# The first modulation of a two-layer backbone, computed chunk by chunk, with three weight tiles in the first product

## The chip, the cores and the metric

One Trainium2 chip, one of its cores, one launch. The time is the device time of one execution in microseconds; three executions of the kernel before gave 1885.32, 1886.90 and 1889.01 us, a median of 1886.9 us. A core has five engines that run at once and wait for each other by semaphores: TensorE (PE), VectorE (DVE), ScalarE (ACT), GpSimd (POOL) and SyncE (SP). SyncE and GpSimd issue the loads here, SyncE on the hardware DMA queue and GpSimd on the software one.

## The reference, cut to what matters

Two layers work on 512 latent tokens and 256 context tokens, each of 1024 channels. The part of the first layer that the change touches:

```python
def rms_norm(x, g):
    y = xf * lax.rsqrt(jnp.mean(xf * xf, axis=-1, keepdims=True) + EPS)
    return (y * g.astype(F32)).astype(x.dtype)

def modulate(h, shift, scale):
    return h * (1 + scale) + shift

sh1, sc1, gt1, sh2, sc2, gt2 = split(silu(c) @ w_ada[l] + b_ada[l])      # latent tokens, w_ada: 1024 x 6144
csh1, csc1, ...              = split(silu(c_ctx) @ w_ada[l] + b_ada[l])  # context tokens, the same weights
u  = modulate(rms_norm(x, g_pre_mix[l]), sh1, sc1) @ w_in[l]             # w_in: 1024 x 2816, 22 tiles of 128 columns
uc = modulate(rms_norm(h_ctx, g_pre_mix[l]), csh1, csc1) @ w_in[l]
```

Behind it come four mixers (neighbourhood attention, a Fourier mixer, sliding-window attention, a gated recurrence), an output projection, and a gated feed-forward part. All is float32.

## The kernel before, in words

**Layout.** Channels lie on the partitions, 128 to a chunk, so that the 1024 channels are NC = 8 chunks; the 768 tokens lie along the rows, 512 latent and then 256 context. The transposed stream is in `x`. A weight tile is 1024 x 128: eight blocks of 128 x 128, 512 KB. There are 196 weight tiles in the whole kernel, in one order, `tile_source` says which.

**A product.** Each float32 product is made of three passes of a fast format: ScalarE copies the loaded tile `raw` into `w_hi` (the rounded part, `split_hi`), VectorE subtracts to get `w_lo` (the rest, `split_lo`), and the activations are split likewise in `h_hi` and `h_lo`. TensorE does hi x hi, lo x hi and hi x lo (`passes`), each in two matmuls of 384 tokens: 6 matmuls for one chunk of one tile, 48 for a tile. `raw`, `w_hi` and `w_lo` have RING = 3 slots, and SyncE loads tile k when the product of tile k - 3 is done (`stream`, L423). The products use the PSUM banks `ps[0]` and `ps[1]` in turn. The first two tiles of the first projection are done side by side (`side_by_side`): for each chunk, as soon as it is there, first tile 0, then tile 1. From the third on, a tile is done in one go.

**The first modulation.** Shift and scale of the first norm are 16 units (8 of shift, 8 of scale), each a row block of 128 x 1024 weights. A unit is a reduction on VectorE (`tensor_tensor_reduce`, L1517) of the weights with silu(c), and one with silu(c_ctx): 32 reductions, one after the other, with their main output thrown away in `ps[3]`. The weights come in ADA_FIRST = 8 transfers of two neighbouring units (1 MB each), so the first four transfers are all the shifts and the last four all the scales. SyncE issues c (two transfers, broadcast to all partitions), five of the eight, the first three weight tiles, and then waits until the first half of x is there before it issues the last three (L415). GpSimd issues the constants, waits for the first modulation transfer, and then issues x in two halves, five small tables, and the first two units of the modulation that comes later (`ada_w`, L492 to L503).

**ScalarE at the start** (from L746): silu of c; the first halves of weight tiles 0 and 1; then, when the small tables and x are there, `pre_norm`: eight squares of x, with the sum over channels made by TensorE (L851, `mean_square`), the root (L698, L699), and then for each chunk and each of the two token groups the copy into `h_hi` with the shift added (L713).

**VectorE at the start** (from L1506): the 32 reductions, the second halves of tiles 0 and 1 (L1521), then `pre_norm`: the columns of shift and scale (three small instructions, L1191 and L1202), and eight chunks of scaling into `tmp` (L1211, two instructions a chunk) and of making `h_lo` (L1218, two a chunk). The split of chunk c - 1 comes behind the scaling of chunk c, so that ScalarE can make `h_hi` beside. Then `ada_pair(0)`, which are four reductions of the later modulation units (L1151) and a small copy, and `gate_bounds`, nine small instructions. Then `projections`: for b from 0 to 7, the split of tile b + 2 (L1139) and, up to b = 6, `ada_pair(b + 1)`; then the recurrence's work, in steps that are fixed to the progress of the product (`STEPS`). GpSimd reloads `ada_w` for a pair when the reductions of the pair before have read it (`ada_loads`, L472).

The order on each engine is the order in which the program writes its instructions; nothing reorders them.

Of the kernel before, what the change touches and what calls it, by code (L numbers as in the profile page):

```python
# [20 lines left out]
F32 = mybir.dt.float32  # L21
# [29 lines left out]

RING = 3
N_OUT = NC

# [94 lines left out]
def hybrid_kernel(nc, xT, cvec, wstream, adaT, badaT, gT, rpb, wf, sink, lbT, hgT, dftL, dftC, dftD, rotm,  # L149
                  rope, swamask, namask, lvmask, sqc, out):  # L150
    with ExitStack() as ctx:
# [241 lines left out]
        def tile_source(k):  # L393
# [6 lines left out]
            return k  # L400

        STEPS = [steps_after(l) for l in range(DEPTH)]

# [5 lines left out]
        def _(sp):  # L409
            for v in range(2):  # L410
                sp.dma_start(c_b[:, v], bass.AP(cvec.tensor, v * D, [[0, P], [1, D]])).then_inc(s_cin, 16)
            for k in range(ADA_FIRST):
                if k == ADA_FIRST // 2 + 1:
                    sp.wait_ge(x_ld[0], 16)
                sp.dma_start(first_units(k), adaT[2 * k:2 * k + 2].rearrange("u p d -> p u d")).then_inc(ada_0_ld[k], 16)  # L415
                if k == ADA_FIRST // 2:
                    for u in range(RING):
                        sp.dma_start(raw[:, u], wstream[tile_source(u)]).then_inc(raw_ld[u], 16)
# [48 lines left out]
        def _(pool):  # L467
# [24 lines left out]
            pool.dma_start(consts[:], sqc.rearrange("k p n -> p k n")).then_inc(s_in, 16)  # L492
            pool.wait_ge(ada_0_ld[0], 16)
            for k in range(2):
# [55 lines left out]
        def _(act):  # L550
# [23 lines left out]
            def project(l, b):  # L574


                blk = PROJ_ORDER[b]
                T = block_width(l, blk)
                act.wait_ge(blk_done, 2 * TP[l]["proj"] + b + 1)
                act.activation(as_product(u_t[:, blk, 0:T], T), product_of(ps[b % 2], T),  # L580
                               ACT.Silu if blk >= QD else ACT.Copy).then_inc(bank_free[b % 2], 1)

            def projections(l):
                g0 = 2 * TP[l]["proj"]
                for b in range(N_ALONE):
                    split_hi(g0 + b + 2)
                    project(l, b)
                steps = recurrence(l)
                for b in range(N_ALONE, N_PROJ):
                    for k in range(NC):  # L590
                        if k == NC // 2 and b < N_PROJ - 1:
                            split_hi(g0 + b + 2)
                        for _ in range(STEPS[l][b][k]):
                            next(steps)
                    project(l, b)
                    if b == N_PROJ - 1:
                        split_hi(g0 + b + 2)
                    if PROJ_ORDER[b] == GD + 1:
                        act.preload_act_table_set(ROOT_TABLES)
# [107 lines left out]
            def pre_norm(T, ready):  # L707
                mean_square(x, T, ready)
                for c in range(NC):
                    for lo, hi, v in STREAMS[:2 if T == TOK else 1]:  # L710
                        act.wait_ge(scaled, nn[0] + 1)
                        nn[0] += 1
                        act.activation(h_hi[:, c, lo:hi], tmp[:, c % 2, lo:hi], ACT.Identity,  # L713
                                       bias=col_sh[:, c, v:v + 1]).then_inc(hhi_ready, 1)
# [33 lines left out]
            act.preload_act_table_set(ROOT_TABLES)  # L748
            for u in range(2):
                act.wait_ge(raw_ld[u], 16)  # L750
                act.activation(w_hi[:, u].rearrange("p c n -> p (c n)"), raw[:, u], ACT.Copy).then_inc(w_hi_done, 1)

            for l in range(DEPTH):
                tp, T = TP[l], width[l]
                if l == 0:
                    act.wait_ge(s_in, 16 * 6)
                    act.wait_ge(consts_done, 1)
                    pre_norm(TOK, lambda c: act.wait_ge(x_ld[2 * c // NC], 16))

# [33 lines left out]
        def _(pe):  # L793
            def passes(tile, k, rhs_hi, rhs_lo, T, begin, end):

                u, slot = tile % 2, tile % RING
                for w, r, first, last in ((w_hi, rhs_hi, begin, False), (w_hi, rhs_lo, False, False),
# [4 lines left out]

            def side_by_side(g0, rhs_hi, rhs_lo, kc, T, ready, order):


                for u in range(2):
                    pe.wait_ge(w_lo_done, 2 * g0 + u + 1)
                    pe.wait_ge(bank_free[u], g0 + 1)
                for n, k in enumerate(order):
                    ready(n)  # L810
                    for u in range(2):
                        mm = passes(2 * g0 + u, k, rhs_hi, rhs_lo, T, n == 0, n == kc - 1)
                        if n == kc - 1:
                            mm.then_inc(blk_done, 1)
# [13 lines left out]
            def projections(l, ready):  # L828


                g0 = TP[l]["proj"]
                side_by_side(g0, h_hi, h_lo, NC, TOK, ready, range(NC))
                steps = recurrence(l)
                for b in range(2, N_PROJ):
                    pe.wait_ge(w_lo_done, 2 * g0 + b + 1)
# [291 lines left out]
        def _(dve):  # L1127
# [68 lines left out]
            nrs, nhi, nlo, nm, nx = [0], [0], [0], [0], [0]  # L1196

            def pre_norm(l, sh, sc, g, T):

# [3 lines left out]
                nrs[0] += 1  # L1203
                dve.wait_ge(rstd_ready, nrs[0])
                st = STREAMS[:2 if T == TOK else 1]
                for c in range(NC + 1):
                    if c >= 2:
                        dve.wait_ge(hlo_ready, nlo[0])
                    if c < NC:
                        for lo, hi, v in st:  # L1210
                            dve.scalar_tensor_tensor(tmp[:, c % 2, lo:hi], x[:, c, lo:hi], col_gs[:, c, v:v + 1],  # L1211
                                                     rstd[:, lo:hi], ALU.mult, ALU.mult).then_inc(scaled, 1)
                    if c:
                        for lo, hi, v in st:
# [150 lines left out]
            def projections(l):  # L1365
                g0 = TP[l]["proj"]
                for b in range(N_ALONE):
                    split_lo(2 * g0 + b + 2)
                    if l == 0 and b < N_ALONE - 1:
# [140 lines left out]
            dve.wait_ge(s_cb, 1)  # L1510
            for k in range(2 * ADA_FIRST):
                if k % 2 == 0:
                    dve.wait_ge(ada_0_ld[k // 2], 16)
                for v in range(2):
                    if 2 * k + v:
                        dve.wait_ge(ada_0_done, 2 * k + v)
                    dve.tensor_tensor_reduce(ps[3][:], first_units(k // 2)[:, k % 2], c_b[:, v], 1.0, 0.0, ALU.mult,  # L1517
                                             ALU.add, ada_c[0][:, k, v:v + 1]).then_inc(ada_0_done, 1)
            for u in range(2):
                dve.wait_ge(w_hi_done, u + 1)  # L1520
                dve.tensor_tensor(w_lo[:, u].rearrange("p c n -> p (c n)"), raw[:, u],  # L1521
                                  w_hi[:, u].rearrange("p c n -> p (c n)").bitcast(F32), ALU.subtract)\
                   .then_inc(w_lo_done, 1)
            dve.wait_ge(s_in, 16 * 6)
            for k in range(2):
                dve.wait_ge(x_ld[k], 16)
            dve.wait_ge(ada_0_done, 4 * ADA_FIRST)

            for l in range(DEPTH):
                tp, T = TP[l], width[l]  # L1530
                if l:
                    dve.wait_ge(ada_copied, 41)
                pre_norm(l, SH1, SC1, G_PRE_MIX, TOK)
                if l == 0:
                    ada_pair(0)
# [130 lines left out]
```

## Time and profile before

| what | value |
|---|---|
| median of three runs | 1886.9 us (1885.32 to 1889.01) |
| the profiled execution's own time | 1888.17 us |
| its span in the profile | 1886.3 us |
| TensorE matmul busy | 1721.2 us, 91% |
| VectorE busy | 978.9 us, 52% |
| ScalarE busy | 597.3 us, 32% |
| GpSimd busy | 148.9 us, 8% |
| mean granted TensorE clock | 0.959 of full speed |
| moved by DMA | 178.84 MB, mean 95 GB/s |

The shares are averages over the whole span. The change touches only the first 150 us or so, in which the engines stand otherwise: in the page's first of 40 slices (47 us) VectorE is busy 7 tenths of the time, TensorE 1 tenth, and the DMA engines 8 tenths, at 329 GB/s. Idle time in a row stands in square brackets, with what ended it behind the arrow. A granted clock of 1.00 is 2.4 GHz, 0.50 is 1.2 GHz.

### The profile page before, as it was taken

Reading aid. Unit: us, or ns where it says so; the run is one execution under the profiler, and the core shown is the slowest. Engines: PE = TensorE matmul, PEld = TensorE weight load, DVE = VectorE, ACT = ScalarE, POOL = GpSimd, SP = SyncE. Lnnn points to the kernel's source line nnn. Section 1 sums busy time; section 2 is a strip of 40 time slices with the busy share of each in tenths; the row PEclk is TensorE's granted clock in tenths of the full one; section 3 lists DMA queues with packets and bytes.
Section 4 is the critical chain, followed back from the end, with each engine's and each line's share of the span. In section 5 each row is a group of like instructions: output and inputs, shape, how many; then the busy total and the mean of one; then the engine's idle time right before and its main releaser. Section 6 shows DMA issues by size and latency. Waiting matters only on the chain.

```text
span 1886.3 us, 24628 instructions
## 1 busy us (share of the span) xinstructions
PE 1721.2 (91%) x10460; PEld 1510.4 (80%) x10460; DVE 978.9 (52%) x1603; ACT 597.3 (32%) x796; POOL 148.9 (8%) x186
## 2 busy tenths in 40 slices
PE   2699998899889999999999979899799899999996
PEld 1699986559689999999999959797566587887874
DVE  7978426665475554555654371752852532233334
ACT  2334434442342222221122142543462432332231
POOL 1010001003200000000000400000102000000003
PEclk9799998899999999999999989999889899999998
DMA  8261115212124343443432202114401132332322
GB/s 329 87 200 47 57 38 124 106 44 71 65 67 134 123 127 111 131 127 109 136 120 89 73 17 79 46 57 95 117 1 56 48 97 90 100 91 92 97 90 100
DMA packets 80638, 178.84 MB, mean 95 GB/s; under 512 B 38912, under 2 KB 39424, under 8 KB 80272
## 3 DMA queue, kind: packets, MB, share of 16 engines
q1 hardware_dynamic: 66864, 122.70, 21.2%
q0 software_dynamic: 13664, 54.56, 8.4%
q8 instruction: 83, 1.36, 0.3%
q14 instruction: 27, 0.22, 0.0%
HBM read 175.14 MB, written 2.10 MB: 94 GB/s over the span
## 4 chain that ended last, share of the span: by engine, by line
PE 82%; DVE 11%; DMA 3%; ACT 2%; issue 1%; SPq 1%; DVEq 0%; ACTq 0%
PE psum L800 70%; PE psum L927 2%; PE psum L938 2%; DMA ada_0a<-in_adaT 1%; DVE f_t L1233 1%; DVE s_sb L1279 1%; PE psum L961 1%; PE psum L1019 1%; DVE x L1237 1%; SPq L441 1%; PE psum L851 1%; DVE tmp L1211 1%; PE psum L883 1%; DVE psum L1517 1%; DMA raw<-in_wstream 1%
## 5 line engine op out<-in xcount | busy, mean ns | idle before, releaser
L800 PE MATMUL psum<-h_hi,w_hi 128*128 128x384 f32 (+1 forms) x1872 | 556.0, 356 | 32.3 <-DVE h_lo L1218 26.6
L800 PE MATMUL psum<-h_hi,w_lo 128*128 128x384 f32 (+1 forms) x1872 | 546.6, 351 | 0.0
L800 PE MATMUL psum<-h_lo,w_hi 128*128 128x384 f32 (+1 forms) x1872 | 546.3, 351 | 0.0
L1139 DVE TENSOR_TENSOR w_lo<-raw,w_hi 128x1024 fp32r<-128x1024 f32 x194 | 239.4, 1234 | 384.2 <-ACT w_hi L562 383.2
L800 PEld LDWEIGHTS psum<-h_hi,w_hi 128*128 128x128 f32 x1872 | 342.1, 190 | 59.2 <-issue 31.6
L562 ACT ACTIVATE w_hi<-raw 128x1024 fp32r<-128x1024 f32 x194 | 205.6, 1060 | 506.3 <-DMA raw<-in_wstream 506.1
L800 PEld LDWEIGHTS psum<-h_lo,w_hi 128*128 128x128 f32 x1872 | 345.5, 190 | 19.9 <-issue 0.7
L800 PEld LDWEIGHTS psum<-h_hi,w_lo 128*128 128x128 f32 x1872 | 344.9, 189 | 19.8
L1151 DVE CUSTOM_DVE_ANT_0 psum<-ada_w,c_b 128x1024 f32<-128x1024 f32 x160 | 202.3, 1264 | 12.0 <-DMA ada_w<-in_adaT 3.3
L800 PE MATMUL psum<-hid_hi,w_hi 128*128 128x384 f32 (+1 forms) x528 | 161.9, 361 | 15.5 <-DVE w_lo L1139 13.2
L1179 DVE TENSOR_TENSOR tmp<-tmp,psum 128x768 f32<-128x768 f32 (+1 forms) x44 | 36.1, 821 | 266.0 <-PE psum L800 266.0
L800 PE MATMUL psum<-hid_hi,w_lo 128*128 128x384 f32 (+1 forms) x528 | 160.9, 359 | 0.0
L800 PE MATMUL psum<-hid_lo,w_hi 128*128 128x384 f32 (+1 forms) x528 | 160.9, 359 | 0.0
L800 PEld LDWEIGHTS psum<-hid_hi,w_hi 128*128 128x128 f32 x528 | 98.5, 192 | 27.3 <-DVE w_lo L1139 17.3
L800 PEld LDWEIGHTS psum<-hid_hi,w_lo 128*128 128x128 f32 x528 | 98.9, 192 | 7.3
L800 PEld LDWEIGHTS psum<-hid_lo,w_hi 128*128 128x128 f32 x528 | 98.8, 192 | 7.0
L851 PE MATMUL psum<-sq,consts 128*128 128x512 f32 (+1 forms) x112 | 49.5, 597 | 53.0 <-ACT sq L692 53.0
L472 POOL DMA_DIRECT2D ada_w<-in_adaT x78 | 41.3, 530 | 707.3 <-DVE ada_t L1151 706.7
L851 PEld LDWEIGHTS psum<-sq,consts 128*128 128x128 f32 x112 | 23.5, 224 | 78.6 <-issue 49.7
L486 POOL TENSOR_TENSOR sq<-f_t 128x768 f32<-128x768 f32 (+1 forms) x28 | 41.1, 1467 | 561.6 <-DVE f_t L1166 449.4
L738 ACT ACTIVATE s_sb<-s_sb,nb 128x512 f32<-128x512 f32 (+3 forms) x80 | 56.8, 714 | 47.9 <-DVE nb L1286 33.7
L682 ACT ACTIVATE hid_hi<-tmp 128x768 fp32r<-128x768 f32 (+1 forms) x44 | 32.5, 740 | 120.6 <-DVE tmp L1179 120.6
(167 smaller groups left out, 1451.0 us busy)
## 6 DMA issues: line engine op xcount, KB each, us to landing
raw<-in_wstream SPq DMA_DIRECT2D x196, 512.0 KB, 3.6
ada_w<-in_adaT POOLq DMA_DIRECT2D x80, 512.0 KB, 3.9
ada_0a<-in_adaT SPq DMA_DIRECT2D x6, 1024.0 KB, 14.6
x<-in_xT POOLq DMA_DIRECT2D x4, 1536.0 KB, 14.3
na_r<-in_rpb SPq DMA_DIRECT2D x64, 64.0 KB, 3.5
fn_l<-in_dftL POOLq DMA_DIRECT2D x2, 2048.0 KB, 8.4
ada_0b<-in_adaT SPq DMA_DIRECT2D x2, 1024.0 KB, 19.3
out_xT<-x SPq DMA_DIRECT2D x4, 512.0 KB, 2.8
```

The lines of the kernel that those rows point to most:

```text
L472: pool.dma_start(ada_w[:, u], adaT[2 * ADA_ORDER[q] + (2 * ADA_FIRST + u)]).then_inc(ada_ld[u], 16)
L486: link(pool.tensor_tensor(sq[:, 1 if b == 0 else 0, 0:T], f, f, ALU.mult))
L562: act.activation(w_hi[:, k % RING].rearrange("p c n -> p (c n)"), raw[:, k % RING], ACT.Copy)\
L682: act.activation(hid_hi[:, i, 0:T], tmp[:, 1, 0:T], ACT.Copy).then_inc(hid_hi_done, 1)
L738: act.activation(p, p, ACT.Exp, bias=nb[:, s % 3, j:j + 1], scale=SCALE, accum_out=sums[:, s % 3, j:j + 1]).then_inc(at_p, 1)
L800: mm = pe.matmul(ps[u][:, at:at + hi - lo], w[:, slot, k], r[:, k, lo:hi], start=first, stop=last)
L851: mm = pe.matmul(ps[2][:, lo:hi], ones, sq[:, c % 2, lo:hi], start=c == 0, stop=c == NC - 1)
L927: mm = pe.matmul(dst, q, keys, start=True, stop=True)
L938: mm = pe.transpose(pt_ps[:, n * j + P * c:n * j + P * c + P], s_sb[:, v % 3, j, o:o + P], ident)
L1139: dve.tensor_tensor(w_lo[:, k % RING].rearrange("p c n -> p (c n)"), raw[:, k % RING], w_hi[:, k % RING].rearrange("p c n -> p (c n)").bit ...
L1151: dve.tensor_tensor_reduce(ps[3][:], ada_w[:, u], c_b[:, v], 1.0, 0.0, ALU.mult, ALU.add, ada_t[:, u, v:v + 1]).then_inc(ada_done, 1)
L1179: dve.tensor_tensor(as_product(tmp[:, 1, 0:T], T), as_product(tmp[:, 0, 0:T], T), product_of(ps[1], T), ALU.mult).then_inc(bank_free[1], 1)
```

## The change

A transfer of the first modulation now holds the shift unit and the scale unit of the same chunk, so that a chunk can be modulated when its own transfer has been reduced. VectorE takes reductions and norm in turn: four transfers are reduced, the three first weight tiles split, and the chunks 0 to 3 normed; then two transfers and chunks 4 and 5; then one and chunk 6; then one and chunk 7. The first product handles three tiles side by side instead of two, the third in the bank `ps[2]`, which no tile used before. ScalarE makes the squares and the root ahead of the first parts of the weight tiles, and of three tiles instead of two. GpSimd doesn't wait any more for the first modulation transfer before it loads x, and SyncE doesn't wait for x before the last three modulation transfers.

```diff
+N_FIRST = 3
+        def bank_of(k):
+            return k if k < N_FIRST else k % 2
@@ block.sync
             for k in range(ADA_FIRST):
-                if k == ADA_FIRST // 2 + 1:
-                    sp.wait_ge(x_ld[0], 16)
-                sp.dma_start(first_units(k), adaT[2 * k:2 * k + 2].rearrange("u p d -> p u d")).then_inc(ada_0_ld[k], 16)
+                sp.dma_start(first_units(k), adaT[k:k + NC + 1:NC].rearrange("u p d -> p u d")).then_inc(ada_0_ld[k], 16)
                 if k == ADA_FIRST // 2:
-                    for u in range(RING):
+                    for u in range(N_FIRST):
                         sp.dma_start(raw[:, u], wstream[tile_source(u)]).then_inc(raw_ld[u], 16)
@@ block.gpsimd
             pool.dma_start(consts[:], sqc.rearrange("k p n -> p k n")).then_inc(s_in, 16)
-            pool.wait_ge(ada_0_ld[0], 16)
             for k in range(2):
@@ block.scalar, projections
                 for b in range(N_ALONE):
-                    split_hi(g0 + b + 2)
+                    if l or b + 2 >= N_FIRST:
+                        split_hi(g0 + b + 2)
                     project(l, b)
@@ block.scalar, the start
-            for u in range(2):
-                act.wait_ge(raw_ld[u], 16)
-                act.activation(w_hi[:, u].rearrange("p c n -> p (c n)"), raw[:, u], ACT.Copy).then_inc(w_hi_done, 1)
-
...
-                    pre_norm(TOK, lambda c: act.wait_ge(x_ld[2 * c // NC], 16))
+                    mean_square(x, TOK, lambda c: act.wait_ge(x_ld[2 * c // NC], 16))
+                    for u in range(N_FIRST):
+                        split_hi(u)
+                    normed(TOK)
@@ block.tensor
-                for u in range(2):
+                for u in range(tiles):
                     pe.wait_ge(w_lo_done, 2 * g0 + u + 1)
-                    pe.wait_ge(bank_free[u], g0 + 1)
+                    pe.wait_ge(bank_free[u % 2], g0 + 1)
                 for n, k in enumerate(order):
                     ready(n)
-                    for u in range(2):
+                    for u in range(tiles):
...
-                side_by_side(g0, h_hi, h_lo, NC, TOK, ready, range(NC))
+                first = 2 if l else N_FIRST
+                side_by_side(g0, h_hi, h_lo, NC, TOK, ready, range(NC), first)
@@ block.vector
+            def first_norm():
+                done = 0
+                for k in range(ADA_FIRST):
+                    dve.wait_ge(ada_0_ld[k], 16)
+                    for part in range(2):
+                        for v in range(2):
+                            n = 4 * k + 2 * part + v
+                            if n:
+                                dve.wait_ge(ada_0_done, n)
+                            dve.tensor_tensor_reduce(ps[3][:], first_units(k)[:, part], c_b[:, v], 1.0, 0.0, ALU.mult,
+                                                     ALU.add, ada_c[0][:, (SH1, SC1)[part] + k, v:v + 1])\
+                               .then_inc(ada_0_done, 1)
+                    if k < 3 or k == 4:
+                        continue
+                    if k == 3:
+                        dve.wait_ge(s_in, 16 * 6)
+                        for u in range(N_FIRST):
+                            split_lo(u)
+                        for half in range(2):
+                            dve.wait_ge(x_ld[half], 16)
+                        nrs[0] += 1
+                        dve.wait_ge(rstd_ready, nrs[0])
+                    dve.wait_ge(ada_0_done, 4 * k + 4)
+                    part = slice(done, k + 1)
+                    b = [bada[:, 0, at0 + done:at0 + k + 1].unsqueeze(2).to_broadcast([P, k + 1 - done, 2])
+                         for at0 in (SH1, SC1)]
+                    g = gcol[:, 0, G_PRE_MIX, part].unsqueeze(2).to_broadcast([P, k + 1 - done, 2])
+                    dve.tensor_tensor(col_sh[:, part], ada_c[0][:, SH1 + done:SH1 + k + 1], b[0], ALU.add)
+                    link(dve.tensor_tensor(col_sc[:, part], ada_c[0][:, SC1 + done:SC1 + k + 1], b[1], ALU.add))
+                    link(dve.scalar_tensor_tensor(col_gs[:, part], col_sc[:, part], 1.0, g, ALU.add, ALU.mult))
+                    normed(TOK, done, k + 1)
+                    done = k + 1
...
-                for c in range(NC + 1):
-                    if c >= 2:
+                for c in range(c0, c1 + 1):
+                    if c >= c0 + 2 or c0:
                         dve.wait_ge(hlo_ready, nlo[0])
-                    if c < NC:
+                    if c < c1:
...
-                    if c:
+                    if c > c0:
@@ block.vector, projections
                 for b in range(N_ALONE):
-                    split_lo(2 * g0 + b + 2)
+                    if l or b + 2 >= N_FIRST:
+                        split_lo(2 * g0 + b + 2)
                     if l == 0 and b < N_ALONE - 1:
                         ada_pair(b + 1)
@@ block.vector, the start
-            for k in range(2 * ADA_FIRST):
...
-            for u in range(2):
-                dve.wait_ge(w_hi_done, u + 1)
...
+            first_norm()
...
-                pre_norm(l, SH1, SC1, G_PRE_MIX, TOK)
-                if l == 0:
+                if l:
+                    pre_norm(l, SH1, SC1, G_PRE_MIX, TOK)
+                else:
                     ada_pair(0)
                     gate_bounds()
```

## Rows read from the trace of the kernel before

**Rows 1.** The page's part 4: shares of the chain that ended last.
```profile
PE 82%; DVE 11%; DMA 3%; ACT 2%; issue 1%; SPq 1%; DVEq 0%; ACTq 0%
```

**Rows 2.** The chain in order of time, 0 to 160: start us, length us, what.
```profile
81.99 1.24 DVE w_lo L1139
83.27 53.40 PE psum L800 x294
```

**Rows 3.** Timeline of VectorE: start us, us, engine line op, out<-in xcount [idle before].
```profile
10.20 1.23 DVE L1517 CUSTOM_DVE_ANT_0 psum<-ada_0a,c_b 128x1024 f32<-128x1024 f32 x1 [9.33 <-DMA ada_0a<-in_adaT]
...
15.61 1.23 DVE L1517 CUSTOM_DVE_ANT_0 psum<-ada_0a,c_b 128x1024 f32<-128x1024 f32 x1
...
55.95 0.17 DVE L1191 TENSOR_TENSOR col_sh<-ada_c,bada 128x16 f32<-128x16 f32 x1
...
56.57 2.21 DVE L1211 SCALAR_TENSOR_TENSOR tmp<-x,col_gs,rstd 128x512 f32<-128x512 f32 x4
...
72.14 2.33 DVE L1218 SCALAR_TENSOR_TENSOR h_lo<-tmp,col_sh,h_hi 128x512 fp32r<-128x512 f32 x4
74.50 1.23 DVE L1151 CUSTOM_DVE_ANT_0 psum<-ada_w,c_b 128x1024 f32<-128x1024 f32 x1
...
81.58 0.16 DVE L1504 TENSOR_TENSOR lb<-lbt,lb 128x4 f32<-128x4 f32 x1
...
83.13 1.23 DVE L1151 CUSTOM_DVE_ANT_0 psum<-ada_w,c_b 128x1024 f32<-128x1024 f32 x1
...
88.62 1.22 DVE L1139 TENSOR_TENSOR w_lo<-raw,w_hi 128x1024 fp32r<-128x1024 f32 x1
...
132.69 1.23 DVE L1139 TENSOR_TENSOR w_lo<-raw,w_hi 128x1024 fp32r<-128x1024 f32 x1 [0.89 <-ACT w_hi L562]
```

**Rows 4.** Timeline of TensorE, at full clock: 27 pairs start between these two.
```profile
88.67 0.51 PE L800 MATMUL psum<-h_hi,w_hi 128*128 128x384 f32 x2
...
98.03 0.51 PE L800 MATMUL psum<-h_hi,w_hi 128*128 128x384 f32 x2
```

**Rows 5.** Windows: stretch and its us, busy us of PE, PEld, DVE, ACT, POOL, PEclk, DMA, GB/s.
```profile
83.20:88.00 4.80, 4.73 (x15) 4.73 (x16) 4.59 (x8) 2.04 (x3) 0.53 (x1) 0.50 0.44 137
83.27:135.30 52.03, 52.03 (x288) 52.03 (x288) 46.09 (x73) 12.64 (x14) 7.40 (x14) 0.95 0.62 201
```

**Rows 6.** Timeline of GpSimd at the start: constants, the two of x, last small table.
```profile
1.25 0.92 POOL L492 DMA_DIRECT2D consts<-in_sqc  x1 [0.81 <-POOLq L1659]
10.35 1.53 POOL L496 DMA_DIRECT2D x<-in_xT  x2 [8.18 <-DMA ada_0a<-in_adaT]
...
14.01 0.54 POOL L501 DMA_DIRECT2D hgain<-in_hgT  x1
```

**Rows 7.** DMA queues: packets, MB, share; in 0:6.5, 0:10.05, 14:16, 16:26 (two rows).
```profile
q1 hardware_dynamic: 389, 1.46, 63.2%
...
q1 hardware_dynamic: 731, 2.80, 73.5%
...
q0 software_dynamic: 66, 0.41, 49.5%
...
q0 software_dynamic: 415, 2.45, 61.2%
q1 hardware_dynamic: 418, 1.59, 40.3%
```

**Rows 8.** DMA issues at 14.01 and at 77.4: count, KB each, us to landing.
```profile
hgain<-in_hgT POOLq DMA_DIRECT2D x1, 2.0 KB, 16.0
...
ada_w<-in_adaT POOLq DMA_DIRECT2D x1, 512.0 KB, 4.6
```

**Rows 9.** Timeline of ScalarE: a weight split, the first squares, the root's last step.
```profile
30.20 1.06 ACT L751 ACTIVATE w_hi<-raw 128x1024 fp32r<-128x1024 f32 x1 [20.78 <-DMA raw<-in_wstream]
...
33.72 1.56 ACT L692 ACTIVATE sq<-x 128x768 f32<-128x768 f32 x2
...
48.96 0.84 ACT L699 ACTIVATE rstd<-lnms 128x768 f32<-128x768 f32 x1
```

More of the change, by code:

```diff
@@ L579, in project @@
                 act.wait_ge(blk_done, 2 * TP[l]["proj"] + b + 1)
-                act.activation(as_product(u_t[:, blk, 0:T], T), product_of(ps[b % 2], T),
+                act.activation(as_product(u_t[:, blk, 0:T], T), product_of(ps[bank_of(2 * TP[l]["proj"] + b)], T),
                                ACT.Silu if blk >= QD else ACT.Copy).then_inc(bank_free[b % 2], 1)
@@ L708, in pre_norm, with normed @@
                 mean_square(x, T, ready)
+                normed(T)
+            def normed(T):
                 for c in range(NC):
@@ L794, in passes @@
             def passes(tile, k, rhs_hi, rhs_lo, T, begin, end):
-                u, slot = tile % 2, tile % RING
+                u, slot = bank_of(tile), tile % RING
                 for w, r, first, last in ((w_hi, rhs_hi, begin, False), (w_hi, rhs_lo, False, False),
@@ L801, in passes, with side_by_side @@
                 return mm
-            def side_by_side(g0, rhs_hi, rhs_lo, kc, T, ready, order):
-                for u in range(2):
+            def side_by_side(g0, rhs_hi, rhs_lo, kc, T, ready, order, tiles=2):
+                for u in range(tiles):
                     pe.wait_ge(w_lo_done, 2 * g0 + u + 1)
-                    pe.wait_ge(bank_free[u], g0 + 1)
+                    pe.wait_ge(bank_free[u % 2], g0 + 1)
                 for n, k in enumerate(order):
                     ready(n)
-                    for u in range(2):
+                    for u in range(tiles):
                         mm = passes(2 * g0 + u, k, rhs_hi, rhs_lo, T, n == 0, n == kc - 1)
@@ L831, in projections @@
                 g0 = TP[l]["proj"]
-                side_by_side(g0, h_hi, h_lo, NC, TOK, ready, range(NC))
+                first = 2 if l else N_FIRST
+                side_by_side(g0, h_hi, h_lo, NC, TOK, ready, range(NC), first)
                 steps = recurrence(l)
-                for b in range(2, N_PROJ):
+                for b in range(first, N_PROJ):
                     pe.wait_ge(w_lo_done, 2 * g0 + b + 1)
@@ L1204, in pre_norm, with normed @@
                 dve.wait_ge(rstd_ready, nrs[0])
+                normed(T, 0, NC)
+            def normed(T, c0, c1):
                 st = STREAMS[:2 if T == TOK else 1]
-                for c in range(NC + 1):
-                    if c >= 2:
+                for c in range(c0, c1 + 1):
+                    if c >= c0 + 2 or c0:
                         dve.wait_ge(hlo_ready, nlo[0])
-                    if c < NC:
+                    if c < c1:
                         for lo, hi, v in st:
@@ L1510, in _ @@
             dve.wait_ge(s_cb, 1)
-            for k in range(2 * ADA_FIRST):
[L1512 to L1518, printed above, removed]
-            for u in range(2):
-                dve.wait_ge(w_hi_done, u + 1)
[L1521 to L1527, printed above, removed]
+            first_norm()
             for l in range(DEPTH):
```

## The prediction

> **What bounds the kernel now.** I read the shares of the chain that ended last first. The reader is to see that TensorE carries 82% of it and VectorE 11%: a change at the start is worth what it does to the moment from which TensorE runs without a gap [rows 1]. Then the chain in order of time: from 83.27 us TensorE runs 53.4 us in one piece of 294 matmuls, and what releases it is the second part of one weight tile, written by VectorE at 81.99 (L1139) [rows 2]. So all before 83.27 is set by VectorE, and one number measures the change: when the fourth weight tile (number 3) is through TensorE.
>
> Third, VectorE in order of time [rows 3]. From 10.20 it runs reductions of L1517, four for 1 MB of modulation weights, one such group each 15.61 - 10.20 = 5.4 us; eight groups, then two splits, end at 55.9. Then come the column sums (56.57 - 55.95 = 0.62 us), eight chunks of scaling and splitting (56.57 to 74.47: 2.24 us a chunk), ada_pair(0) and gate_bounds (74.50 to 81.74: 7.24 us), the split of tile 2, ada_pair(1) (83.13 to 88.62: 5.5 us), the split of tile 3. There is hardly a gap: the start is a queue of VectorE work, and its order decides.
>
> Fourth, TensorE. Side by side it takes tiles 0 and 1 while the chunks come, and stops before 83.27. A pair of matmuls takes (98.03 - 88.67)/27 = 0.347 us [rows 4], a tile of 24 pairs 8.32 us. The six tiles 2 to 7 took 52.03 us, 2.1 more than 6 x 8.32, and the row of the stretch after the restart shows a granted clock of 0.50 [rows 5]: half of full speed (1.2 GHz of 2.4) after the pause that [rows 2] ends. So now tile 2 ends at 83.27 + 10.4 = 93.7, tile 3 at 102.0.
>
> **The change part by part, on the profile's own time axis.**
>
> *Loads.* GpSimd no longer waits for the first modulation transfer, so the two transfers of x follow the constants at 1.25 + 0.92 = 2.2 us instead of 10.35, 8.15 earlier [rows 6]. SyncE no longer waits for x either. The bytes are the same; only who goes first changes. Transfers of x issued at 10.35 show up in the queue's bytes in the slice 14 to 16 us, with half of it, so about 4 us after issue; now from about 6.5. While both queues have work, the software queue moves 2.45 MB and the hardware queue 1.59 MB in 10 us: 0.245 and 0.159 MB/us [rows 7]. The last small table was issued at 14.01 and took 16.0 us; ScalarE needs all of them before it squares. Shifted by 8.15 it lands at 30.0 - 8.15 = 21.9 [rows 6, 8].
>
> The modulation chunks pay for it. Chunk 0 landed just before 10.20 [rows 3], when the hardware queue had moved 2.80 MB; the 1 MB of c and the chunk are 2, so a landing comes 0.8 MB late. Now 1.46 MB are through at 6.5, and 0.159 MB/us from there give chunk 0 at 6.5 + 1.34/0.159 = 14.9, chunk 1 at 21.2. The software queue's 4.3 MB (x 3.1, first ada_w tiles 1.05, tables) are through at 24.0; alone at 0.40 the hardware queue lands chunk 2 near 25.4 and chunk 3 near 27.9 [rows 7]. VectorE at 5.4 a chunk: 14.9 to 20.3, 21.2 to 26.6, to 32.0, to 37.5. It starts 4.7 late and has a gap of about 0.9.
>
> That row can be read in two ways. In it both queues moved as many packets, 415 and 418, but not as many bytes [rows 7]. The Trainium skill (DMA: Bandwidth & Descriptors, "Queues, rings and completion order") says that each DMA engine goes round its queues packet by packet; by that rule x keeps its advantage from the start, and the split by bytes that I used holds; by even bytes x would come 3 us later (a rival below). The trace agrees with the rule.
>
> *Order on ScalarE.* The squares now come ahead of the weight splits. The squares, their sums on TensorE and the root took 33.72 to 49.80 = 16.1 us, cold matmuls included [rows 9]. From 21.9 that ends at 38.0. Then three splits of 1.06 us [rows 9]: tile 0's first part is there at 39.05, the last by 41.0. VectorE has stood since 37.5, 1.6 us. Its three second parts (1.14 apart) end at 42.55. The weights themselves have long landed (before at 30 to 33 behind the same bytes), so nothing hides here but the wait for x.
>
> *Norm in four stretches.* From 42.55: columns 0.62 and chunks 0 to 3 at 2.24: 52.1. Chunks 4 and 5: reductions 10.8, columns 0.62, two chunks 4.5: 68.1. Chunk 6: 5.4 + 0.62 + a single chunk. A single one cannot overlap with its neighbour: 1.15 scaling + 1.14 split + ScalarE's part between. At least it costs the 2.24 of a chunk, at most 1.15 + 1.12 + 1.14 = 3.4; I take 2.8, since the narrow half overlaps: 76.9. Chunk 7 the same: 85.7. Before, the last chunk was ready at 74.47 [rows 3]: 11 us later, of which late start and stalls 7.2 (4.7 + 0.9 + 1.6), the third split moved ahead 1.1, three more sets of columns 1.9, bubbles 1.2; rounding the rest.
>
> *Three tiles side by side.* TensorE has 9 pairs a chunk, 3.1 us warm. It is idle before chunks 4 and 7 for 4 us and more, so it meets chunk 7 at half clock: (about 7 x 0.64 + 2 x 0.347) = 5.2, the 0.64 from the 2.1 us that seven pairs lost. Tiles 0, 1, 2 end at 91.0; before, tile 2 ended at 93.7. That is the gain that the change holds, 2.7 us, if the next tile is ready.
>
> *What the next tile waits for.* It is not. In the new order VectorE does after chunk 7: ada_pair(0) and gate_bounds 7.24: 92.95; the split in front of ada_pair(1) has gone, for tile 2 is split already; ada_pair(1), whose first weights land 4.6 us after an issue that follows the pair's start by 2.9, so 0.25 of wait [rows 8]: 93.2 to 98.7; only then tile 3's split, and TensorE 1.28 us after its start [rows 2]: 100.0. Beside it, hidden: the load of raw 3 is issued when tile 0 ends (about 87.9), lands by 93, ScalarE splits it by 94. If VectorE were free that would be the next thing late: 94 + 1.3 = 95.3. TensorE has idled 9 us, and restarts at half clock: tile 3 ends at 100.0 + 10.4 = 110.4.
>
> *After it* all is as before. Tiles 4 to 7 follow each 8.32; VectorE needs 132.69 - 88.62 = 44.1 us from tile 3's split to tile 9's, TensorE 52.03 - 8.32 = 43.7 from tile 3 to tile 8 with the restart; so VectorE is just in time, with under 1 us of slack where the recurrence starts [rows 3, 5]. Layer 1 is unchanged.
>
> **Sum.** Tile 3 ends at 110.4 instead of 102.0: +8.4 us. The profiled execution took 1888.17 (span 1886.3), so 1896.6 for one like it; it stands 1.3 above the median of 1886.9, so the median becomes 1895.3. 0.2% (3.8 us) is what a measurement here can tell from no change. Bounds: if VectorE alone set the pace (chunk 0 at 10.2, x in time), three splits would end at 10.2 + 21.7 + 3.5 = 35.4, 7.1 earlier: +1.3; with a warm restart besides, -0.8. If x lands 4 us later than I say: +12.4.
>
> **Rivals.**
> *The start is not slowed* (not slower): x and the chunks both come early enough that VectorE never stands. For it: the whole load of 14.6 MB is unchanged, and VectorE, not the queue, is the slower one now. Against: the root needs x by 35.4 - 3.5 - 16.1 = 15.8, that is nearly all of the bandwidth from 6.5 on, and then chunk 0 is late by the same bytes. Price: +1.3, so 1888.2. It decides if both ScalarE has its root and VectorE its fourth group by 32.
> *TensorE sets the end and gains*: tile 3's split would be ready by 91.0, 2.7 to 3 us faster: 1884. Against: ada_pair(1) stands before the split, and even the best start gives 92.9.
> *The queues share evenly by bytes*: 3.3 MB until x and the tables are in takes 16.3 us at 0.202 instead of 13.5 at 0.245, some 3 us later for ScalarE, while VectorE has its chunks earlier: +11.4, so 1898.3. Against: the row says otherwise.
> *Later work gives some back*: a wait behind tile 8 that is not tied to TensorE absorbs part, say half: +4.2, 1891.1. Against: all loads there are released by finished tiles.
>
> **How the numbers follow.** Forecast (+8.4, with sizes off by up to 2.5): 0.70. Even bytes or x later: 0.12. Later work gives back: 0.06. Start not slowed: 0.08. TensorE gains: 0.04. Slower by over 0.2%: 0.70 + 0.12 + half of the 0.06 = 0.85; within: 0.08 + 0.03 = 0.11; faster: 0.04. The range from 1889 to 1899.5 leaves out the faster case and the start that is hardly slowed, and the far end of late x.
>
> **What would show it.** In the new profile: chunk 0's first reduction near 15; ScalarE's first square near 22, its last root near 38; VectorE standing before its first split (near 37 to 39); reductions and scalings in turn until 85.7; then ada_pair(0), the gates and ada_pair(1) ahead of tile 3's split near 98.7; TensorE idle from 91 to 100 with that split as what ended it, clock 0.50 after it. Wrong would be: a first square before 18, the last chunk before 80, or tile 3 starting before 95.

## The result, and the profile after

The changed kernel takes 1895.3 us (median of five, 1892.4 to 1896.1) against 1886.9 (five, 1885.3 to 1889.0): ratio 1.0040, 95% interval [1.0026, 1.0055]. The medians differ by 8.4 us, as forecast to a tenth; the interval of the ratio allows anything from 4.9 to 10.4 us, so the tenth means nothing. The agreement is partly luck besides: the traces show a first stage that lost 12.5 us where 8.4 were forecast, and about 4 us that came back later.

The profiled execution took 1895.34 us (span 1893.5), which is the median itself. VectorE in order of time; columns as in [rows 3]:

```profile
12.53 1.23 DVE L1216 CUSTOM_DVE_ANT_0 psum<-ada_0a,c_b 128x1024 f32<-128x1024 f32 x1 [11.66 <-DMA ada_0a<-in_adaT]
...
18.88 1.23 DVE L1216 CUSTOM_DVE_ANT_0 psum<-ada_0a,c_b 128x1024 f32<-128x1024 f32 x1 [1.09 <-DMA ada_0a<-in_adaT]
...
41.10 3.50 DVE L1146 TENSOR_TENSOR w_lo<-raw,w_hi 128x1024 fp32r<-128x1024 f32 x3 [6.13 <-ACT w_hi L565]
...
53.95 1.23 DVE L1216 CUSTOM_DVE_ANT_0 psum<-ada_0a,c_b 128x1024 f32<-128x1024 f32 x1
...
75.37 1.15 DVE L1256 SCALAR_TENSOR_TENSOR tmp<-x,col_gs,rstd 128x512 f32<-128x512 f32 x2
76.98 1.15 DVE L1263 SCALAR_TENSOR_TENSOR h_lo<-tmp,col_sh,h_hi 128x512 fp32r<-128x512 f32 x2 [0.46 <-ACT h_hi L720]
78.16 1.23 DVE L1216 CUSTOM_DVE_ANT_0 psum<-ada_0b,c_b 128x1024 f32<-128x1024 f32 x1
...
86.72 1.23 DVE L1158 CUSTOM_DVE_ANT_0 psum<-ada_w,c_b 128x1024 f32<-128x1024 f32 x1
...
94.06 1.23 DVE L1158 CUSTOM_DVE_ANT_0 psum<-ada_w,c_b 128x1024 f32<-128x1024 f32 x1
...
99.73 1.23 DVE L1158 CUSTOM_DVE_ANT_0 psum<-ada_w,c_b 128x1024 f32<-128x1024 f32 x1 [3.05 <-DMA ada_w<-in_adaT]
...
102.46 1.22 DVE L1146 TENSOR_TENSOR w_lo<-raw,w_hi 128x1024 fp32r<-128x1024 f32 x1
...
147.46 1.22 DVE L1146 TENSOR_TENSOR w_lo<-raw,w_hi 128x1024 fp32r<-128x1024 f32 x1
...
150.02 0.96 DVE L1465 COPY hv<-psum 128x768 f32<-128x768 f32 x1
```

The reader is to see the brackets: 2.3 us later at the start, 1.09 for the second chunk, 6.13 before the first split, and 3.05 in the middle of ada_pair(1), which I had not in the sum. The last row is the recurrence's first work on VectorE. Before, it stood at 137.46 behind 2.24 us of waiting for TensorE; now it comes 12.6 later, straight behind the queue. The same row before:

```profile
137.46 0.96 DVE L1419 COPY hv<-psum 128x768 f32<-128x768 f32 x1 [2.24 <-PE psum L1031]
```

ScalarE beside it, as in [rows 9]: the squares start 10.1 us earlier than before, and the root is what the splits wait for.

```profile
23.64 1.58 ACT L696 ACTIVATE sq<-x 128x768 f32<-128x768 f32 x2 [13.71 <-DMA hgain<-in_hgT]
...
39.21 0.84 ACT L703 ACTIVATE rstd<-lnms 128x768 f32<-128x768 f32 x1
39.95 2.93 ACT L565 ACTIVATE w_hi<-raw 128x1024 fp32r<-128x1024 f32 x3
```

TensorE, as in [rows 4]: tile 2 in the kernel before, then chunk 7 of the three tiles and tile 3 in the changed one.

```profile
83.27 1.01 PE L800 MATMUL psum<-h_hi,w_hi 128*128 128x384 f32 x2 [4.49 <-DVE w_lo L1139]
```

```profile
86.74 1.01 PE L806 MATMUL psum<-h_hi,w_hi 128*128 128x384 f32 x2 [5.16 <-DVE h_lo L1263]
...
103.73 1.01 PE L806 MATMUL psum<-h_hi,w_hi 128*128 128x384 f32 x2 [11.10 <-DVE w_lo L1146]
```

Windows of the changed kernel, as in [rows 5]: from the restart at 103.73 the clock is 0.50 for some 5.5 us, and so it was from 86.7 on.

```profile
86.70:92.00 5.30, 5.26 (x16) 5.26 (x17) 5.07 (x8) 0.00 (x0) 0.53 (x1) 0.50 0.45 152
...
103.73:109.20 5.47, 5.47 (x17) 5.47 (x18) 4.96 (x8) 0.00 (x0) 0.53 (x1) 0.50 0.49 158
```

The prediction named one number, the end of tile 3 on TensorE. SyncE issues its next weight load then, here before and after: 12.5 us later, where 8.4 was forecast.

```profile
102.38 0.33 SPq L423 DMA_DIRECT2D raw<-in_wstream  x1
```

```profile
114.89 0.33 SPq L427 DMA_DIRECT2D raw<-in_wstream  x1
```

### The profile page after: what moved, and what is told of

Same layout as the page of the kernel before. It is cut to its first block, busy times and chain, and to the rows that moved or that the text cites. A ratio compares the mean times of both kernels' runs of the same rounds, so it can differ in the third digit from the quotient of the medians.

```text
span 1893.5 us, 24643 instructions
## 1 busy us (share of the span) xinstructions
PE 1722.5 (91%) x10460; PEld 1511.7 (80%) x10460; DVE 980.0 (52%) x1612; ACT 597.0 (32%) x796; POOL 149.0 (8%) x186
## 4 chain that ended last, share of the span: by engine, by line
PE 82%; DVE 11%; ACT 2%; DMA 2%; issue 1%; SPq 1%; POOL 0%; DVEq 0%; ACTq 0%; POOLq 0%
PE psum L806 69%; PE psum L934 2%; PE psum L945 2%; PE psum L858 2%; DVE f_t L1278 1%; DVE s_sb L1324 1%; PE psum L968 1%; PE psum L1026 1%; DVE psum L1216 1%; DMA hgain<-in_hgT 1%; DVE x L1282 1%; SPq L445 1%; DVE w_lo L1146 1%; DVE psum L1158 1%; PE psum L890 1%
```

## The experiments

In this table "recurrence" is the start of VectorE's first copy into `hv`, and "tile 16" how much later than in the first profile of the kernel before VectorE split weight tile 16 (207.1 us there), by which time the first steps of the recurrence are through.

| kernel | median us (runs) | ratio to before | recurrence | tile 16 |
|---|---|---|---|---|
| before, profiled first | 1886.9 | | 137.46 | 0 |
| before, again | 1886.6 (12) | 1.0007 [0.9997, 1.0017] | 138.36 | +0.9 |
| changed | 1895.3 (5) | 1.0040 [1.0026, 1.0055] | 150.02 | +12.5 |
| changed, again | 1895.5 (5) | 1.0046 [1.0029, 1.0063] | 150.36 | +12.2 |
| a: split 3 first | 1892.7 (9) | 1.0033 [1.0018, 1.0047] | 150.68 | +8.2 |
| b: five groups | 1891.3 (10) | 1.0027 [1.0017, 1.0037] | 145.26 | +6.5 |
| c: two tiles | 1894.1 (7) | 1.0040 [1.0025, 1.0055] | 147.81 | +10.3 |
| e: x late | 1901.1 (5) | 1.0078 [1.0064, 1.0093] | 154.63 | +16.4 |
| g: weights behind ada_w | 1892.8 (5) | 1.0033 [1.0021, 1.0045] | 149.96 | +8.9 |
| j: b and g | 1889.1 (11) | 1.0015 [1.0006, 1.0024] | 146.00 | +5.8 |
| d: before, loads early | 1890.1 (11) | 1.0013 [1.0003, 1.0023] | 140.58 | +3.1 |
| f: before, third split early | 1883.5 (11) | 0.9986 [0.9977, 0.9994] | 138.31 | -0.6 |
| k: f, gates first | 1885.7 (12) | 0.9996 [0.9987, 1.0006] | 139.44 | +2.0 |
| l: k, split 3 first | 1882.2 (12) | 0.9980 [0.9969, 0.9992] | 140.72 | -0.2 |

The intervals of a, b, c and g overlap those of the changed kernel, whose ten executions lie between 1892.1 and 1898.9 us; b's lie between 1888.8 and 1894.4. Only e and j are clear of it by their intervals, so what a, c and g are worth is read mainly from the traces.

**What the early x costs and brings.** Experiment e puts one wait back into the changed kernel:

```diff
             pool.dma_start(consts[:], sqc.rearrange("k p n -> p k n")).then_inc(s_in, 16)
+            pool.wait_ge(ada_0_ld[0], 16)
```

> The changed kernel with GpSimd waiting again for the first modulation transfer before it loads x. Theory 1 (x and the small tables set the root, the root sets the splits, and VectorE stands for it): chunk 0's reduction starts at 10.2 instead of 12.5, the first square near 32 instead of 23.6, VectorE stands from 32 to 49, and the time rises by about 8 us. Theory 2 (the early x is what slows the start, by taking half of the bandwidth): the time falls by 2 to 3 us.

```profile
9.60 1.23 DVE L1217 CUSTOM_DVE_ANT_0 psum<-ada_0a,c_b 128x1024 f32<-128x1024 f32 x1 [8.73 <-DMA ada_0a<-in_adaT]
...
45.81 1.23 DVE L1147 TENSOR_TENSOR w_lo<-raw,w_hi 128x1024 fp32r<-128x1024 f32 x1 [14.71 <-ACT w_hi L566]
```

Chunk 0 comes 2.9 us earlier and helps nothing; VectorE stands 14.71 us for the root, the splits are 4.7 later, and the median rises by 5.7. Theory 1 in kind; I had said 8, but the first square came at 29.7, not 32. So with the new order on ScalarE x has to come early. Experiment d takes the two waits out of the kernel before and leaves its order:

```diff
-            pool.wait_ge(ada_0_ld[0], 16)
...
-                if k == ADA_FIRST // 2 + 1:
-                    sp.wait_ge(x_ld[0], 16)
```

> The kernel before with one part of the change: GpSimd does not wait for the first modulation transfer, nor SyncE for x. Order of work, transfers and two tiles side by side stay. Theory 1 (the early x costs the first chunks what the change's trace shows, a start at 12.5 instead of 10.2 and 1.1 us more of waiting, less the 0.6 us gap that goes): about 2.8 us slower, all of it ahead of tile 2. Theory 2 (with x early ScalarE and the loads are ready sooner and this pays): no change or faster.

The first reduction starts at 12.83 and tile 2 at 86.39, 3.1 later than in [rows 2]; the median is 3.4 above the kernel before's 1886.7 (by the interval 0.6 to 4.3). The early x alone costs about what theory 1 said, in a kernel whose VectorE doesn't stand for the root.

**Where VectorE stands.** Experiment b:

```diff
-                    if k < 3 or k == 4:
+                    if k < 4:
                         continue
-                    if k == 3:
+                    if k == 4:
```

> The changed kernel with one edit: five groups of reductions instead of four before the first splits and norms (chunks 0 to 4, then 5, 6 and 7 singly). VectorE stood 6.1 us before the first split in the changed kernel, for ScalarE's root. Theory 1 (that stand is paid in full, all after it is one queue): 5.4 us of reductions fit into it, less 0.5 for one more single chunk, so 4.9 us faster, and the recurrence starts at 145. Theory 2 (TensorE's restarts or the ada_w loads set the pace behind it): under 2 us faster.

```profile
41.48 2.36 DVE L1146 TENSOR_TENSOR w_lo<-raw,w_hi 128x1024 fp32r<-128x1024 f32 x2 [1.19 <-ACT w_hi L565]
...
145.26 0.96 DVE L1465 COPY hv<-psum 128x768 f32<-128x768 f32 x1
```

The stand falls from 6.13 to 1.19 and the recurrence starts 4.8 earlier, where 4.9 was said; the median falls by 4.1. VectorE's stand is paid in full in the first stage.

**The second unit of ada_pair(1).** In the changed kernel it is issued at 92.39 and lands 7.3 us later, while SyncE issues three weight tiles (89.06, 90.98, 92.67), since three tiles end within 4 us. Experiment g, in SyncE's `stream`:

```diff
                     sp.wait_ge(blk_done, k - RING + 1)
+                    if k == RING + 1:
+                        sp.wait_ge(ada_ld[1], 32)
```

> The changed kernel with one edit: SyncE loads weight tile 4 (and 5 behind it) only when the second unit of ada_pair(1) has landed. Theory 1 (the three weight loads that the three finished tiles release within 4 us hold this unit up, it took 7.3 us to land and VectorE stood 3.05 us): the unit lands in 4.5 to 5 us, VectorE's wait there falls under 0.5 us, tile 3's split comes near 99.5 instead of 102.46, and the first stage is 2.5 to 3 us shorter. Theory 2 (the unit is late because GpSimd issues it late, at 92.39, whatever else is in flight): no change.

DMA issue of that unit in the kernel before, in the changed kernel, then in g (count, KB, us to landing):

```profile
ada_w<-in_adaT POOLq DMA_DIRECT2D x1, 512.0 KB, 5.1
```

```profile
ada_w<-in_adaT POOLq DMA_DIRECT2D x1, 512.0 KB, 7.3
```

```profile
ada_w<-in_adaT POOLq DMA_DIRECT2D x1, 512.0 KB, 3.8
```

```profile
99.24 1.22 DVE L1148 TENSOR_TENSOR w_lo<-raw,w_hi 128x1024 fp32r<-128x1024 f32 x1
...
102.30 1.23 DVE L1160 CUSTOM_DVE_ANT_0 psum<-ada_w,c_b 128x1024 f32<-128x1024 f32 x1 [1.84 <-issue]
```

The wait is gone and the split comes at 99.24 (102.46 in the changed kernel, 98.7 in the prediction). With the loads of tiles 4 and 5 held back the unit lands in half the time, so the transfers compete, and that is the missing term. VectorE's queue gets most of it back in later waits for `ada_w`, the recurrence starts where it did (149.96), yet tile 16 is 3.6 earlier: TensorE's lead counts also when VectorE's start does not move. The median is 2.6 lower, within the intervals. Experiment j has both edits, b and g.

> The changed kernel with two edits together: five groups of reductions ahead of the first norm, and weight tiles 4 and 5 loaded only behind the second unit of ada_pair(1). Theory 1 (the two are separate entries in one queue on VectorE, and add): 4.0 and 2.6 us off the changed kernel's median, so about 1888.7, 2 us above the kernel before. Theory 2 (one hides the other): not better than the better of the two, 1891.3.

1889.1, against 1888.7 if they add: the median favours theory 1, though b's and j's intervals overlap. The changed kernel with its two stands mended is still 0.15% slower than before. By the terms of the sum the rest would be the late start of the first splits, three more sets of columns, and short idle gaps; no run separates them.

**TensorE's wait or VectorE's queue.** Experiment a, in VectorE's `projections`:

```diff
-                    if l or b + 2 >= N_FIRST:
+                    if l:
                         split_lo(2 * g0 + b + 2)
+                    elif b < N_ALONE - 1:
+                        split_lo(b + 3)
                     if l == 0 and b < N_ALONE - 1:
                         ada_pair(b + 1)
```

> The changed kernel with one edit: VectorE splits tile 3 ahead of ada_pair(1), and every later tile of the eight ahead of its pair. Theory 1 (TensorE's wait for tile 3, 11.1 us in the changed kernel, is what the end pays): the split follows ScalarE's at 94.8, TensorE starts tile 3 at 96.1 instead of 103.73, and the time falls by about 7.6 us. Theory 2 (VectorE's whole queue up to the recurrence is the bound, since it came there at 149.99 and TensorE at 149.18, so that both are tied): TensorE gets to tile 8 7 us earlier but VectorE begins the recurrence at about 150 as before, TensorE's wait moves there, and the time falls by 0 to 2 us.

```profile
96.83 1.01 PE L806 MATMUL psum<-h_hi,w_hi 128*128 128x384 f32 x2 [3.59 <-DVE w_lo L1146]
...
142.44 0.82 PE L1038 MATMUL psum<-consts,u_t 128*128 128x128 f32 x6
```

```profile
150.68 0.96 DVE L1467 COPY hv<-psum 128x768 f32<-128x768 f32 x1
```

TensorE reaches the recurrence 6.6 us earlier, VectorE no earlier, and the result is neither theory's: 4.3 us by tile 16, 2.7 in the median. In the recurrence TensorE waits 2.2 us for VectorE once, where the changed kernel has no such wait, so a part of the lead is lost there. My reading, which no run tests by itself: the lead is product work that is done and not owed when VectorE's steps come, and is worth a part of itself. Experiment c goes back to two tiles (`N_FIRST = 2`, with RING weight tiles still loaded at the start).

> The changed kernel with two tiles side by side instead of three, all else the same. Theory 1 (the third tile puts tile 3's split behind two pairs, and three weight loads at once hold up ada_pair(1) by 3.05 us): tile 2 starts at 94.2 and the tiles then follow, tile 8 at 146.2 instead of 149.2, VectorE's wait of 3.05 us for ada_w is gone, and the time falls by 2 to 3 us. Theory 2 (the third tile is worth the 2.7 us that TensorE gains by it): the time rises by 2 to 3 us.

```profile
94.15 1.01 PE L806 MATMUL psum<-h_hi,w_hi 128*128 128x384 f32 x2 [4.54 <-DVE w_lo L1146]
...
147.81 0.96 DVE L1465 COPY hv<-psum 128x768 f32<-128x768 f32 x1 [1.96 <-PE psum L1038]
```

Tile 2 starts at 94.15 as said, the wait for `ada_w` is gone, the first stage is 2.2 shorter; the median is 1.2 lower, within both intervals. No gain of the third tile shows, and its cost is not resolved by times.

**What of the change is worth keeping.** Experiment f puts only the third split ahead of the norm, in the kernel before:

```diff
-            for u in range(2):
+            for u in range(3):
                 act.wait_ge(raw_ld[u], 16)
...
-            for u in range(2):
+            for u in range(3):
                 dve.wait_ge(w_hi_done, u + 1)
```

(and in `projections` on both engines the split at b = 0 of layer 0 is left out).

> The kernel before with one edit: ScalarE and VectorE split tile 2 together with tiles 0 and 1, ahead of the norm, so that TensorE need not wait from 78.8 to 83.3. Theory 1 (TensorE's wait is the price): tile 2 follows at once at 79.6 without a restart at half clock, tile 3's split comes at 88.4 behind ada_pair(1), tile 8 starts 4 us earlier, 4 us faster. Theory 2 (VectorE's queue up to the recurrence is the other bound, with 2.2 us of slack where it waited for TensorE at 137.46): at most 2.2 us faster.

```profile
83.35 0.98 PE L801 MATMUL psum<-h_hi,w_hi 128*128 128x384 f32 x2 [2.76 <-ACT u_t L580]
```

The split was in time, but TensorE stood all the same: ScalarE's copy of tile 0 out of its bank was queued behind the exponential that `gate_bounds` releases (82.30). Still it is the first version that beats both: 0.9986, or 2.6 us. Experiment k calls `gate_bounds` ahead of `ada_pair(0)`; l also has a's order of splits.

> The kernel before with the third weight split ahead of the norm, as in f_before_third_split_early, and gate_bounds ahead of ada_pair(0) on VectorE. In that run TensorE stood 2.8 us before tile 2, not for the split but for ScalarE's copy of tile 0 out of its bank, which was queued behind the small exponential that gate_bounds releases. Theory 1 (TensorE's earlier progress pays, as where tile 3's split was put first in the changed kernel): TensorE goes through at 80.6, without 2.8 us of standing and about 2 us of restart, and the time is 2 to 4 us below that run's 1883.5. Theory 2 (VectorE's queue to the recurrence, which starts at 138.3 in that run without waiting for TensorE, is the bound): no change from 1883.5.

> As k_gates_first, and each split of the eight ahead of its pair on VectorE (tile 3's ahead of ada_pair(1)). Theory 1: TensorE has tile 3 in time at 89 as well (in k it waits about 2 us for a split at 90 and restarts at half clock), so another 2 to 4 us, 1878 to 1881. Theory 2 (VectorE's queue is the bound): VectorE stands about 1.5 us for ScalarE before that split, the recurrence starts that much later, and it is not faster than k, or 1 us slower.

Timeline of TensorE in k, then the window 79 to 131 us of l (columns as in [rows 5]):

```profile
93.10 1.01 PE L801 MATMUL psum<-h_hi,w_hi 128*128 128x384 f32 x2 [5.03 <-DVE w_lo L1140]
```

```profile
79.00:131.00 52.00, 52.00 (x300) 51.76 (x300) 42.01 (x65) 15.11 (x16) 6.90 (x13) 1.00 0.63 203
```

In k the wait moved on: ada_pair(1) now follows so soon that it stands 3.5 us for its weights, tile 3's split comes at 91.8, and TensorE stands 5 us for it. Neither theory had that, and the median is 2.1 above f's (1885.7), though the intervals overlap. In l TensorE runs from tile 0 into the recurrence without a gap and at full clock, and it is the fastest: 1882.2, ratio 0.9980 [0.9969, 0.9992]; 3.8 us by the ratio, against f's 2.6, whose interval overlaps. It is 3.5 us below k, as theory 1 said, and misses its 1878 to 1881.

Where that gain lies is another matter. TensorE reaches the recurrence 5.5 us earlier than before (first row, then l), but there it waits for VectorE, 2.4 us in the longest wait:

```profile
136.51 0.82 PE L1031 MATMUL psum<-consts,u_t 128*128 128x128 f32 x6
```

```profile
131.05 0.82 PE L1032 MATMUL psum<-consts,u_t 128*128 128x128 f32 x6
...
156.00 0.73 PE L1020 MATMUL psum<-hq,hs 64*64 64x64 f32 x24 [2.44 <-DVE hd L1446]
```

A weight load that SyncE issues at 166.65 there came at 166.82 before. By tile 16 the lead is still 0.2 us, and f's is 0.6, less than the 0.9 by which two traces of one kernel differ there. Both are 4 to 5 us ahead only at tile 80. So the times show that f and l are faster, and the traces that TensorE's stands at the start are gone or shorter; that the one makes the other is not shown.

**Later parts.** The two unchanged kernels were profiled a second time.

> The kernel before, unchanged, profiled once more. The first trace compared with that of the change shows a loss of 12.5 us at the start of the recurrence but only 7.2 over the span. Theory 1 (the rest is drawn anew in each execution by TensorE's restarts): up to the recurrence this trace agrees with the first within 0.5 us, and behind it drifts from it by 1 to 5 us in steps of about 1. Theory 2 (something behind the recurrence really gives 5 us back in the changed kernel): this trace keeps to the first within 1 us all along.

> The changed kernel, unchanged, profiled once more. Theory 1 (the first stage is fixed by the program and the tail is drawn anew): the recurrence starts within 1 us of 150.0 again, while the time from there to the end differs from the first profile's 1743.5 by up to 5 us; the median stays near 8 us over the kernel before. Theory 2 (the tail of the changed kernel is really shorter): again 1743 to 1745, against 1748.8 and 1752.2 in the two profiles of the kernel before.

Both first stages repeat, within 1.1 and 0.4 us. Behind them the second profile of the kernel before drifted from its first in steps, up and down, to 4.3 at the last weight tile, and its execution took 1892.44, 5.8 above its median; the changed kernel's second took 1898.94 against 1895.34. In eight of the twelve experiments the profiled execution is the slowest of its set. So a single profile can't price a change by its span: 7.2 us from the first pair, 6.5 from the second, but 10.8 or 2.9 crosswise. Yet the medians differ by 8.2 to 8.9 where the first stages differ by about 12, so 3 to 4 us are given back by the medians; the interval of the first measurement (up to 10.4) leaves some 1.5 or more, that of the second (up to 11.9) next to nothing. One piece shows in all four traces, the stretch behind tile 23's split up to tile 24's. Before (first, second), then changed (first, second):

```profile
296.00:431.50 135.50, 118.06 (x826) 80.24 (x827) 97.39 (x282) 65.96 (x135) 8.55 (x18) 0.89 0.25 79
```

```profile
297.00:433.00 136.00, 118.07 (x827) 80.30 (x828) 97.87 (x283) 65.97 (x135) 8.55 (x18) 0.89 0.25 78
```

```profile
308.50:442.60 134.10, 117.15 (x827) 79.62 (x828) 97.08 (x283) 65.83 (x135) 8.55 (x18) 0.90 0.25 80
```

```profile
308.50:442.60 134.10, 116.79 (x828) 79.59 (x829) 97.47 (x283) 65.83 (x135) 8.56 (x18) 0.92 0.25 79
```

The same matmuls are busy about 1 us less there, at a clock about a hundredth or more higher, and from split to split it is 1.3 to 1.6 us shorter than in the kernel before. But f, k and l, which keep the order of the kernel before, shorten the same stretch by 1.3, 2.3 and 1.5 us, while a, a version of the changed kernel, keeps its length within 0.1. So the new order of reductions and norm is not needed to shorten it. Why it is shorter, and where the other 2 us are, stays open.

## Why the prediction was right, and where it was not

*What bounds the start.* Right: VectorE's queue, and moving its stands and waits moves the end of tile 3 (b, e, g). Up to the first split, though, the chain of x, squares and root has taken over from that queue. (A slip ahead of the prediction: in the page's first slice TensorE is busy 2 tenths, not 1; nothing hangs on it.)

*Loads.* Right in kind, mis-sized both ways. Chunk 0 came at 12.5 instead of 14.9; the late start and gap cost VectorE 2.8 (2.3 + 1.1 - 0.6), not the 5.6 of the sum. Its 0.8 MB of lateness came from a stretch in which the hardware queue was nearly alone; that it does not carry over to two mixed queues is my guess. The last small table took 17.8 us to land instead of 16.0, so the squares started at 23.64, not 21.9.

*Order on ScalarE.* The chain of root and splits took what it was given (38.0 forecast, 40.05 measured, the 1.7 being the table's). The stand was 6.13 instead of 1.6, because VectorE was done at 35.0, not 37.5, and the root later. Late start and stand make up for each other, since the split waits for the root whatever VectorE does ahead of it: an earlier chunk 0 would only have made the stand longer. The first split was due at 39.05 and came at 41.10, chunk 7 was due at 85.7 and ready at 86.7.

*Norm in four stretches.* Right: a single chunk is 78.16 - 75.37 = 2.8 us, with 0.46 of waiting for ScalarE.

*Three tiles.* TensorE was through at 103.73 - 11.10 = 92.6 (forecast 91.0), 1.4 earlier than the kernel before with its third tile (SyncE's next load at 92.67 instead of 94.06); the gain was lost to the wait for tile 3's split, as forecast.

*What the next tile waits for.* Right in order, wrong in one term: "so 0.25 of wait" for ada_pair(1)'s weights, with the 4.6 us of [rows 8] taken over. That is the first unit, and it came in time (4.2 us, no wait). The second unit, issued 2.8 us later, was not in the sum; before, it had taken 5.1 and been in time. With three weight loads around it it took 7.3, and the wait was 3.05. TensorE started tile 3 at 103.73 instead of 100.0. That is the largest miss of the first stage, and g shows it.

*The sum.* At the end of tile 3 the loss was 12.5 us instead of 8.4: 1.0 from the last chunk, 2.8 from that wait, the rest small. "After it all is as before" failed too, by the 3 to 4 us above, and so the total came out: a mechanism that was right, with a first stage sized too small and a give-back that was not in it, which cancel. The rival that later work gives some back had been given 0.06. Its effect, and about its size, stand beside the forecast; that a wait absorbs it, as it said, is not shown.

## What to carry to other kernels

When one engine's queue sets a stage, write down its stands before and after: here 2.3 + 1.1 + 6.1 + 3.1 us of new standing account for most of the loss, and filling the 6.1 with work that was due anyway (b) left 1.2 of it and lowered the median by 4.1. Ask of each stand what ended it, too: the first three add up to one wait for the root, so mending the late start alone would bring nothing. Work that frees several buffers at once also launches several transfers at once, and the transfer that the next step needs competes with them (g). Before adding a tile to the front of a product, look at what the next tile waits for. The versions that came out faster (f, l) have the third split ready early and only two tiles side by side. And follow a lead beyond the stage in which it was won: l's 5.5 us were down to 0.2 some 35 us later.

## What the runs showed of the hardware

A 512 KB load of the software queue took 3.8 us to land when the only weight load beside it landed 0.1 us after its issue (g), 4.8 to 6.1 with two weight loads issued in the 3.4 us before it (c 4.8, the kernel before 5.1, k 6.1), and 7.3 with three issued from 3.3 us before it to 0.3 after (the changed kernel). TensorE stood 4.5, 5.2 and 11.1 us and each time came back at a granted clock of 0.50; after the 2.8 us of f it was 0.50 too, from 83.35 to 85.00. In l TensorE ran 52 us without a gap at 1.00. And two profiles of one kernel, alike within 1.1 us over their first 280 us, were 4.3 us apart in span.
